# Router products by row tile inside the output projection, and earlier loads of the first four experts' weights, in a one-core streaming encoder layer

## The chip, the core and the metric

The kernel runs on one core of one Trainium2 chip. A core has a matrix engine (TensorE, PE in the profile), three elementwise engines (VectorE or DVE, ScalarE or ACT, GpSimd or POOL), and a sync engine (SyncE, SP) that here only issues transfers. Each has its own instruction queue and they meet at semaphores. The core has 16 DMA engines between HBM and the on-chip memory (SBUF); products land in PSUM, whose eight banks hold 512 fp32 columns each. The metric is the device time of one execution in microseconds, lower is better. All data is fp32.

## The reference

One encoder layer for 528 prompt rows (16 learned meta rows and 512 new ones) and 32 sample rows; two attention branches run ahead of what follows. The change is in the last part of it:

```python
def layer_tail(x, o_sb, o_dsa, g_sb, g_dsa, w_sb_branch, w_dsa_branch, w_out, norm2_g, ...):
    merged = (g_sb * (o_sb.reshape(B, L, SB_WIDTH) @ w_sb_branch)
              + g_dsa * (o_dsa.reshape(B, L, DSA_WIDTH) @ w_dsa_branch))
    h = x + merged @ w_out                       # w_out 1024 x 1024
    return h + hier_moe(rms_norm(h, norm2_g), ...)

def hier_moe(h, w_group, w_router, w_gate, w_up, w_down):
    group_probs = softmax(xt @ w_group)          # 4 groups, the best one is taken
    elog = xt @ w_router                         # 32 experts, the best 2 of 8 in that group
    ...                                          # weights of the two experts of each row
    a, b = xt @ w_gate[e], xt @ w_up[e]          # per expert 1024 x 256 each
    hh = silu(a) * b * comb
    y += hh @ w_down[e]                          # 256 x 1024
```

The meta rows are dropped from the result, so this part runs over 544 rows: 512 prompt rows in four tiles of 128, and one tile of 32 sample rows. The 32 experts' weights are 3 MiB each (gate 1 MiB, up 1 MiB, down two halves of 512 KiB), 96 MiB in all, and each is read once.

## The kernel before

The order of the work is written out by hand, engine by engine, with semaphores between.

**End of the attention.** TensorE fills the sparse attention's steps with 32 products of the gates and of one branch (`branch_products`, L1078, counted by `gd_ready`, 48 in all), then runs the sparse branch's projection (`by_width`, 16 jobs). DVE gates and adds them into `merged` (`merged_ready` counts 16). POOL then issues the loads of the residual rows X (`xres_in`) and of the norm gains `g2b` (`g2_in`).

**Output projection and second norm.** For each row tile t of 128 rows TensorE runs two jobs of 8 products, `merged` turned as the stationary operand and half of `w_out` (512 columns) as the moving one (`pj_job`, L747); the 32-row tile is packed four wide (L1218). Jobs go round four PSUM banks (`pj_wait_free`, the table `PJ` says which engine empties which job). DVE adds each job onto X (L2033, L2040, then `h_ready`), ACT squares and sums the row (L1547, `ss2_ready`), POOL takes the inverse root (L1620, L1621, `rstd2_ready`), and DVE writes the normed rows into `x2row` (L2020, `x2_ready`), a pair of buffers. DVE's program has the norm of tile t-1 behind the adds of tile t. TensorE turns the normed rows (`tr_job`, L737, two jobs of four transposes), with a lag of two tiles: tile u = t-2 behind the projection of tile t. ACT copies them into `xT`, which holds all 544 rows (L1355).

**Router.** When tile 3 is turned, one product runs over 512 rows at once: `wr` (36 columns: 4 groups, 32 experts) stationary, `xT` moving (L747). Another does the 32 sample rows. Their result has the experts on the partitions, so ACT copies it to `lgT` (L1557), TensorE turns it back (L1239), and ACT copies it to `rl` (L1560, `logits_ready`). DVE then picks groups and experts and builds lists of rows (L2070 to L2155), TensorE counts positions and makes the index lists (L1247 to L1256), and POOL gathers the first expert's rows (L1746).

**Experts.** Rows go through the experts in blocks of 64. For expert n, TensorE turns the gathered rows (L1266), multiplies with gate and up (L1273, `gu_ready`), turns the hidden rows (L1279) and multiplies with down (L1284, `y_done`). Weights sit in `MS` = 6 slots. SP loads expert n >= 6 into its slot when expert n-6 has left it: gate and up (L680) after `gu_ready` of n-6, the two down halves (L684) after `y_done` of n-6. The first six are loaded earlier: expert 0 behind `w_out` (L557) after the attention (`pvd_done`), expert 1 after `merged_ready`, experts 2 to 4 when the output projection is done, expert 5 after `logits_ready`, its last half after `slots_ready`.

Of the kernel before, what the change touches and what calls it, by code (L numbers as in the profile page):

```python
# [25 lines left out]
D = 1024  # L26
# [23 lines left out]
MS = 6  # L50
# [185 lines left out]
def build(nc, a, out):  # L236
    ctx = ExitStack()
    with ctx:
# [83 lines left out]
        moe_w = [arena[:, s * SLOT:(s + 1) * SLOT] for s in (2, 3, 0, 1)]  # L322

        Xg = ring_w[0:CAP, 0:2 * D].rearrange("p (i d) -> p i d", i=2)
        Yb = ring_w[:, 2 * D:3 * D].rearrange("p (i d) -> p i d", i=2)
        xgT = ring_w[:, 3 * D:4 * D].rearrange("p (i k s) -> p i k s", i=2, k=KT)

        moe_gu = [w[:, 0:4096] for w in moe_w] + [arena[:, 4 * SLOT:4 * SLOT + 4096], xnT[:, 0:4096]]
        moe_dn = [[w[:, 4096 + D * j:4096 + D * (j + 1)] for j in range(2)] for w in moe_w]
        moe_dn += [[ring_w[:, (6 + j) * D:(7 + j) * D] for j in range(2)], [ring_w[:, 5 * D:6 * D], tabs[:, 0:D]]]  # L330
        hid = ring_w[:, 4 * D:4 * D + 256].rearrange("p (i c) -> p i c", i=2)
        sil = ring_w[:, 4 * D + 256:4 * D + 512].rearrange("p (i c) -> p i c", i=2)
        hidT = ring_w[:, 4 * D + 512:4 * D + 768].rearrange("p (i c) -> p i c", i=2)
        lgT = tabs[:, 640:1200]

        x2row = ring_w[:, 0:2 * D].rearrange("p (i d) -> p i d", i=2)
        g2b = ring_w[:, 2 * D:3 * D]
        scrap = ring_w[:, 3 * D:4 * D]
# [28 lines left out]
        at_slot = ring_w[:, 0:2 * NT * CAP].rearrange("p (c s) -> p c s", s=CAP)  # L367
        at_block = ring_w[:, 640:640 + 2 * NT * NBLK].rearrange("p (c b) -> p c b", b=NBLK)
# [103 lines left out]
        logits_ready = sem("logits_ready")  # L472
# [41 lines left out]
        chunk_at = [wslot[s] for s in slots] + [arena[:, 0:4096], arena[:, 4096:8192]]  # L514


        pj_used = {0: 5, 1: 10, 2: 15, 3: 20, 4: 28, 5: 36, 9: 52, 12: 61, 13: 61}
# [5 lines left out]
        held_by = {2: 0, 3: 1, 4: 2, 5: 3, 6: 4, 7: 5, 8: 6, 10: 7, 11: 8, 9: 10}  # L523
# [40 lines left out]
        PJ = ["dve"] * 15 + ["act"] * (NT + 16) + ["dve"] * 16 + ["dve"] * 9 + ["act"] * 2  # L564
        J_IQ, J_SM, J_DQ, J_SV, J_SK, J_SQ = 0, 5, 10, 15, 20, 28
        J_B, J_WO, J_RT = 36, 52, 61

        TR = ["dve"] * 10 + ["act"] * 8 + ["act"] * 20 + ["act"] * 11
# [24 lines left out]
        RG = [(0, SEQ), (SEQ, NTOK)]  # L593
# [5 lines left out]
        def _(sp):  # L599
# [87 lines left out]
            for n in range(NE):  # L687
                s = n % MS
                if n == 1:
                    sp.wait_ge(merged_ready, 16)  # L690
                if n == 2:
                    sp.wait_ge(pj_ready, pj_used[13])
                if n == 5:
                    sp.wait_ge(logits_ready, 1)
                if n >= MS:
                    sp.wait_ge(gu_ready, n - MS + 1)
                load_gate_up(s, n, gu_in[s])
                if n >= MS:
                    sp.wait_ge(y_done, n - MS + 1)
                for j in range(2):  # L700
                    if n == 5 and j:
                        sp.wait_ge(slots_ready, 1)
                    load_down(s, n, j, dn_in[s])
# [23 lines left out]
        def _(pe):  # L727
# [477 lines left out]
            for t in range(NT + 2):  # L1205
# [17 lines left out]
                u = t - 2  # L1223
                if u >= 0:
# [4 lines left out]
                    if u >= NT - 2:  # L1229

# [560 lines left out]
        def _(dve):  # L1791
# [8 lines left out]
            for p in pairs:  # L1800
                link(nc.vector.memset(p[:, :], 0.0))
# [441 lines left out]
```

## Time and profile before

| | us |
|---|---|
| median of 3 runs | 937.8 |
| lowest, highest | 935.15, 939.65 |
| the profiled execution | 936.06 |
| its span | 934.3 |

| stretch, us from the span's start | what runs |
|---|---|
| up to 545.9 | projections, both attentions, branch projections |
| 545.9 to 606.5 | output projection |
| 606.5 to 625.6 | last turns, router |
| 625.6 to 656.9 | choice of experts, index lists, first gather, first gate and up product |
| 656.9 to 890.5 | experts, until the last weights have landed |
| 890.5 to the end | last two experts, scatter, sum, store |

The profiled execution took 936.06 us, of which the span from the first to the last instruction is 934.3 us. TensorE is busy for 827.5 us of it; the mean granted TensorE clock is 0.958 of full speed. The share of busy time is a mean over stages with different limits; which wait ends last has to be read stage by stage.

### The profile page before, as it was taken

To read this page: it belongs to the slowest core of one execution; us is meant where nothing else is said; L and a number is where in the kernel's file an instruction comes from. 1 tells how busy PE (TensorE), PEld (TensorE's weight loads), DVE (VectorE), ACT (ScalarE), POOL (GpSimd) and SP (SyncE) were. 2 spreads that over 40 slices of the span, in tenths; PEclk is the share of its full clock that TensorE was granted. 3 is DMA by queue.
4 is the path that set the end of the run, shared out by engine and by line. 5 is a ranking of instruction groups with operands and counts; after the bars stand their busy time and mean duration, and the time that the engine had idled before them with its cause. 6 is when DMAs were issued, how large, how long until landed. Compare 5 with 4: busy or idle time off the path is not lost.

```text
span 934.3 us, 11345 instructions
## 1 busy us (share of the span) xinstructions
PE 827.5 (89%) x4438; PEld 505.5 (54%) x4438; DVE 306.3 (33%) x788; ACT 224.0 (24%) x461; POOL 187.9 (20%) x257
## 2 busy tenths in 40 slices
PE   5999999999999998999999999953999988777870
PEld 3464344787666755766666854522555545444530
DVE  4213657996544421223222622235000000000005
ACT  3021331112333332343333500120122211111110
POOL 2223420000423212000000020101244332233230
PEclk9999999999999999999999999975999999999995
DMA  8424020422102001202040851195799999999927
GB/s 284 136 91 121 2 91 1 140 102 87 43 0 85 8 1 38 59 3 89 0 91 2 313 231 45 46 387 201 276 395 391 389 394 381 395 388 396 388 77 290
DMA packets 52422, 160.13 MB, mean 171 GB/s; under 512 B 14032, under 2 KB 16304, under 8 KB 43632
## 3 DMA queue, kind: packets, MB, share of 16 engines
q1 hardware_dynamic: 45184, 145.34, 42.0%
q0 software_dynamic: 7184, 14.06, 4.4%
q8 instruction: 35, 0.57, 0.3%
q14 instruction: 19, 0.16, 0.1%
HBM read 151.35 MB, written 15.86 MB: 179 GB/s over the span
## 4 chain that ended last, share of the span: by engine, by line
PE 70%; DMA 11%; SPq 6%; DVE 4%; POOL 3%; ACT 2%; issue 2%; POOLq 0%; DVEq 0%; ACTq 0%
PE quad L747 24%; PE pair L1078 9%; DMA arena<-in_w_up 6%; PE pair L941 5%; PE pair L1273 4%; PE quad L1273 3%; PE quad L815 3%; DMA xnT<-in_w_up 3%; SPq L680 3%; SPq L684 3%; PE quad L1284 2%; PE pair L737 2%; PE quad L1035 2%; POOL arena L1705 1%; PE pair L862 1%
## 5 line engine op out<-in xcount | busy, mean ns | idle before, releaser
L1273 PE MATMUL quad<-arena,ring_w 128*64 128x256 f32 x512 | 65.4, 413 | 16.5 <-DMA arena<-in_w_up 15.8
L747 PE MATMUL quad<-ring_w,xnT 128*128 128x512 f32 (+1 forms) x192 | 79.4, 554 | 0.0
L1750 POOL DMA_INDIRECT y_d<-ring_w,idx_y x64 | 57.7, 901 | 70.5 <-ACT ring_w L1584 58.4
L941 PE MATMUL pair<-xnT,ring_w 128*128 128x272 f32 x256 | 70.3, 410 | 0.9 <-POOLq L1711 0.9
L1078 PE MATMUL pair<-xnT,ring_w 128*128 128x272 f32 x256 | 65.8, 403 | 0.0
L1273 PEld LDWEIGHTS quad<-arena,ring_w 128*64 128x64 f32 x512 | 41.9, 149 | 35.3 <-issue 20.9
L747 PE MATMUL quad<-xnT,ring_w 128*128 128x280 f32 (+1 forms) x256 | 60.6, 396 | 0.0
L1746 POOL DMA_INDIRECT ring_w<-xn_d,idx_x x32 | 30.9, 966 | 137.4 <-PE pair L1266 53.7
L747 PE MATMUL quad<-arena 128*128 128x512 f32 x128 | 55.4, 593 | 1.2 <-DVEq L2012 1.2
L941 PEld LDWEIGHTS pair<-xnT,ring_w 128*128 128x128 f32 x256 | 46.4, 192 | 16.7 <-issue 7.9
L1078 PEld LDWEIGHTS pair<-xnT,ring_w 128*128 128x128 f32 x256 | 46.5, 189 | 15.3 <-issue 6.9
L747 PEld LDWEIGHTS quad<-xnT,ring_w 128*128 128x128 f32 x256 | 48.2, 190 | 11.3 <-issue 0.8
L1989 DVE CUSTOM_DVE_ANT_0 arena<-quad,arena 128x528 f32<-128x528 f32 (+4 forms) x34 | 17.7, 520 | 103.9 <-PE quad L1133 60.9
L747 PEld LDWEIGHTS quad<-ring_w,xnT 128*128 128x128 f32 x192 | 34.3, 189 | 31.7 <-issue 26.1
L1273 PE MATMUL pair<-arena,ring_w 128*64 128x256 f32 x352 | 42.1, 393 | 8.5 <-DMA arena<-in_w_up 8.1
L1921 DVE MAX8 small<-arena 128x8 f32<-128x544 f32 (+4 forms) x81 | 45.0, 555 | 2.2
L1923 DVE MATCH_REPLACE8 arena<-small,arena 128x544 f32<-128x544 f32 (+4 forms) x81 | 43.5, 537 | 0.0
L747 PEld LDWEIGHTS quad<-arena 128*128 128x128 f32 x128 | 24.2, 190 | 31.3 <-issue 29.7
L1273 PEld LDWEIGHTS pair<-arena,ring_w 128*64 128x64 f32 x352 | 27.1, 141 | 20.1 <-issue 8.7
L1730 POOL DMA_DIRECT2D hreg<-in_x_prompt x4 | 2.1, 536 | 173.6 <-DVEq L2012 173.6
L1078 PE MATMUL pair<-hreg,ring_w 128*128 128x272 f32 x128 | 33.0, 404 | 1.9 <-ACT arena L1498 1.8
L1948 DVE TENSOR_SCALAR arena<-quad 128x288 f32<-128x288 f32 (+6 forms) x22 | 16.0, 726 | 56.7 <-issue 37.9
(254 smaller groups left out, 1174.0 us busy)
## 6 DMA issues: line engine op xcount, KB each, us to landing
arena<-in_w_gate SPq DMA_DIRECT2D x27, 1024.0 KB, 16.9
arena<-in_w_up SPq DMA_DIRECT2D x27, 1024.0 KB, 25.4
arena<-in_w_down SPq DMA_DIRECT2D x44, 512.0 KB, 17.7
ring_w<-in_w_in SPq DMA_DIRECT2D x8, 2048.0 KB, 8.2
ring_w<-in_w_down SPq DMA_DIRECT2D x15, 512.0 KB, 17.9
xnT<-in_w_gate SPq DMA_DIRECT2D x5, 1024.0 KB, 17.7
xnT<-in_w_up SPq DMA_DIRECT2D x5, 1024.0 KB, 26.6
arena<-in_w_out SPq DMA_DIRECT2D x2, 2048.0 KB, 11.0
```

Source lines behind the costliest of these rows:

```text
L680: sp.dma_start(moe_gu[slot][:, n * 2048:(n + 1) * 2048], w[bass.ds(e * P, P), :])\
L684: sp.dma_start(moe_dn[slot][j], wd[:, bass.ds(e * 2 + j, 1), :].rearrange("p o c -> p (o c)"))\
L737: last = nc.tensor.transpose(b[0:cols, i * n:i * n + src.shape[0]], src, idn)
L747: last = nc.tensor.matmul(o, l, r, start=i == 0, stop=i == len(mms) - 1)
L815: last = nc.tensor.matmul(bank[t], xT[:, k, N_META + P * t:N_META + P * (t + 1)], chunk8(0)[:, k, :], start=k == 0, stop=k == KT - 1)
L941: last = nc.tensor.matmul(bank[6 + job % 2][:, 0:hi - lo], chunk8(6 + cb // 4)[:, k, c0:c0 + P], xT[:, k, lo:hi], start=k == 0, stop=k == ...
L1078: last = nc.tensor.matmul(bank[6 + job % 2][:, 0:hi - lo], w[:, k, c0:c0 + P], rhs[:, k, lo:hi], start=k == 0, stop=k == kt - 1)
L1273: last = nc.tensor.matmul(bank[4 * q + 1][64 * f:64 * f + 64, 0:256].rearrange("p (g c) -> p g c", g=2), xgT[:, q, k, :], wv[:, :, k, P * ...
L1746: pool.indirect_dma_start(Xg[:, q, :], None, xn2_d, bass.IndirectOffsetOnAxis(ap=rows, axis=0), bounds_check=NTOK - 1, oob_is_err=False).t ...
L1750: pool.indirect_dma_start(y_d, bass.IndirectOffsetOnAxis(ap=rows, axis=0), Yb[64 * c:64 * c + 64, q, :], None, bounds_check=4 * NTOK - 1, ...
L1921: link(nc.vector.max(top8, v))
L1923: link(nc.vector.match_replace(v, top8, v, TAKEN))
```

## The change

- TensorE's loop over the tiles is written anew. Behind the projection of tile t stands first the router product of tile t-2 (`routed`), then the turning of tile t-1: the turning lags one tile instead of two. The router product now has the turned rows stationary and `wr` (36 columns) moving, so that rows come out on the partitions; it is five jobs, one for each tile. The two wide products, the copies to `lgT` and the five transposes back are gone.
- The turned rows go into a pair of buffers `x2T` instead of `xT`. ACT copies each router result straight into `rl`.
- ACT's squares are written to a PSUM pair instead of SBUF. DVE sets the unused part of `rl` to zero at the start of the program.
- `w_out` is loaded into `xnT` and the first half of `ring_w`, when the gate products are done with them (`held_by`), instead of into the arena. Gate and up of experts 0 to 3 follow after `pvd_done`; their down halves when the branch projection is done, five of the eight after `merged_ready`; experts 4 and 5 when the output projection is done. From expert 6 on the waits are as before.
- `x2row`, `g2b` and small buffers of the expert loop move within `ring_w` and `tabs`.

The core of the diff:

```diff
-        chunk_at = [wslot[s] for s in slots] + [arena[:, 0:4096], arena[:, 4096:8192]]
+        chunk_at = [wslot[s] for s in slots] + [xnT[:, 0:4096], wslot[0]]
...
-        held_by = {2: 0, 3: 1, 4: 2, 5: 3, 6: 4, 7: 5, 8: 6, 10: 7, 11: 8, 9: 10}
+        held_by = {2: 0, 3: 1, 4: 2, 5: 3, 6: 4, 7: 5, 8: 6, 10: 7, 11: 8, 9: 10, 12: 11, 13: 11}
...
-            for n in (7, 8, 10, 11, 9):
+            for n in (7, 8, 10, 11, 9, 12, 13):
                 load_chunk(sp, n)
-            sp.wait_ge(pvd_done, NT)
-            load_chunk(sp, 12)
-            load_chunk(sp, 13)
...
+            sp.wait_ge(pvd_done, NT)
+            for n in range(4):
+                load_gate_up(n, n, gu_in[n])
+            sp.wait_ge(pj_ready, pj_used[9])
+            for n in range(4):
+                for j in range(2):
+                    if (n, j) == (1, 1):
+                        sp.wait_ge(merged_ready, 16)
+                    load_down(n, n, j, dn_in[n])
+            sp.wait_ge(pj_ready, pj_used[13])
+            for n in range(4, MS):
+                load_gate_up(n, n, gu_in[n])
+                for j in range(2):
+                    load_down(n, n, j, dn_in[n])
...
-            for t in range(NT + 2):
+            def routed(t):
+
+                pe.wait_ge(tr_free_act, emptied(TR, "act", T_X2 + 2 * t + 1))
+                pj_job([(x2T[:, t % 2, k, 0:TOK[t]], wr[:, k, :]) for k in range(KT)], lambda b: b[0:TOK[t], 0:36])
+
+            for t in range(NT + 1):
...
-                u = t - 2
-                if u >= 0:
+                if t == 2:
+                    pe.wait_ge(wr_in, 32)
+                if t >= 2:
+                    routed(t - 2)
+                if t >= 1:
+                    u = t - 1
                     pe.wait_ge(x2_ready, u + 1)
...
+            routed(NT - 1)
...
-                    link(nc.scalar.activation(scrap[0:r, :], X[0:r, t, :], ACT.Square, scale=1.0 / 32.0,
+
+                    link(nc.scalar.activation(pair67[0:r, :], X[0:r, t, :], ACT.Square, scale=1.0 / 32.0,
...
-            dve.wait_ge(logits_ready, 1)
+            dve.wait_ge(pj_free_act, emptied(PJ, "act", J_RT[NT - 1]))
```

TensorE's queue from the output projection to the router, before. `quad<-arena 128x512` is the projection (48 are the six jobs of tiles 0 to 2), `pair<-cst,ring_w` the turning of normed rows, `quad<-xnT,small` the router:

```order
L747 MATMUL quad<-arena,ring_w 128x272 x64
L747 MATMUL quad<-arena 128x512 x48
L737 MATMUL pair<-cst,ring_w 128x128 x8
L747 MATMUL quad<-arena 128x512 x16
L737 MATMUL pair<-cst,ring_w 128x128 x8
L1218 MATMUL quad<-arena 32x256 x32
L737 MATMUL pair<-cst,ring_w 128x128 x16
L747 MATMUL quad<-xnT,small 36x512 x8
L737 MATMUL pair<-cst,ring_w 128x32 x8
L747 MATMUL quad<-xnT,small 36x32 x8
L1239 MATMUL pair<-cst,tabs 128x36 x4
L1239 MATMUL pair<-cst,tabs 32x36
```

The same place in the changed program, from the second half of tile 1's projection to the turning of tile 2. The projection of a tile is now a row of 8 that reads `xnT` and one that reads `ring_w`; `quad<-small,ring_w` is a router product:

```order
L745 MATMUL quad<-ring_w,arena 128x512 x8
L735 MATMUL pair<-cst,ring_w 128x128 x8
L745 MATMUL quad<-xnT,arena 128x512 x8
L745 MATMUL quad<-ring_w,arena 128x512 x8
L745 MATMUL quad<-small,ring_w 128x36 x8
L735 MATMUL pair<-cst,ring_w 128x128 x8
L745 MATMUL quad<-xnT,arena 128x512 x8
L745 MATMUL quad<-ring_w,arena 128x512 x8
L745 MATMUL quad<-small,ring_w 128x36 x8
L735 MATMUL pair<-cst,ring_w 128x128 x8
```

The turning of tile 0 stands between the projections of tiles 1 and 2, where there was nothing, and two router products stand ahead of the last projection. The end of the same stretch, changed program, from the last products of the 32-row tile on:

```order
L1221 MATMUL quad<-ring_w,arena 32x256 x2
L745 MATMUL quad<-small,ring_w 128x36 x8
L735 MATMUL pair<-cst,ring_w 128x128 x8
L745 MATMUL quad<-small,ring_w 128x36 x8
L735 MATMUL pair<-cst,ring_w 128x32 x8
L745 MATMUL quad<-small,ring_w 32x36 x8
L1242 MATMUL quad<-rt,cst 128x192
```

Behind the last projection there are now three router products and the turning of two tiles, before three tiles were turned there and the wide router products followed. SP's queue from `w_out` to the last load that is not yet under the loop's waits, before:

```order
L557 DMA arena<-in_w_out 128x8x512 [waits pvd_done]
L557 DMA arena<-in_w_out 128x8x512
L680 DMA arena<-in_w_gate 128x2048
L680 DMA arena<-in_w_up 128x2048
L684 DMA arena<-in_w_down 128x1024 x2
L680 DMA arena<-in_w_gate 128x2048 [waits merged_ready]
L680 DMA arena<-in_w_up 128x2048
L684 DMA arena<-in_w_down 128x1024 x2
L680 DMA arena<-in_w_gate 128x2048 [waits pj_ready]
```

and in the changed program, from the fourth expert's gate on:

```order
L672 DMA arena<-in_w_gate 128x2048
L672 DMA arena<-in_w_up 128x2048
L676 DMA arena<-in_w_down 128x1024 [waits pj_ready]
L676 DMA arena<-in_w_down 128x1024 x2
L676 DMA arena<-in_w_down 128x1024 [waits merged_ready]
L676 DMA arena<-in_w_down 128x1024 x4
L672 DMA arena<-in_w_gate 128x2048 [waits pj_ready]
L672 DMA arena<-in_w_up 128x2048
L676 DMA ring_w<-in_w_down 128x1024 x2
L672 DMA xnT<-in_w_gate 128x2048
```

Two experts' weights are now left for the time after the output projection, where there were four.

## Rows read from the trace of the kernel before

**Rows 1.** Windows: us, busy (x) of PE, PEld, DVE, ACT, POOL, PEclk, DMA share, GB/s.
```profile
650.00:656.00 6.00, 5.31 (x33) 3.28 (x34) 0.00 (x0) 0.60 (x1) 0.94 (x1) 0.58 0.13 38
656.00:662.00 6.00, 5.57 (x49) 3.58 (x45) 0.58 (x2) 0.87 (x2) 0.93 (x1) 1.00 0.71 246
662.00:668.00 6.00, 6.00 (x47) 3.39 (x45) 0.58 (x2) 1.47 (x3) 2.03 (x3) 1.00 0.73 233
656.90:890.50 233.60, 204.77 (x1430) 120.32 (x1430) 17.36 (x60) 43.54 (x89) 79.28 (x86) 0.97 1.00 383
```
**Rows 2.** SP's timeline: start us, us, what it issues.
```profile
656.91 0.33 SPq L680 DMA_DIRECT2D arena<-in_w_gate  x1
...
665.18 0.80 SPq L684 DMA_DIRECT2D arena<-in_w_down  x2
```
**Rows 3.** TensorE's timeline, branch projection to router; in brackets idle before and releaser.
```profile
515.25 29.50 PE L747 MATMUL quad<-arena,ring_w 128*128 128x272 f32 x128
545.93 41.47 PE L747 MATMUL quad<-arena 128*128 128x512 f32 x96 [1.18 <-DVEq L2012]
587.23 1.04 PE L737 MATMUL pair<-cst,ring_w 128*128 128x128 f32 x8
588.11 13.90 PE L747 MATMUL quad<-arena 128*128 128x512 f32 x32
...
602.82 3.66 PE L1218 MATMUL quad<-arena 128*32 128x256 f32 x64
606.41 1.16 PE L737 MATMUL pair<-cst,ring_w 128*128 128x128 f32 x8
610.47 1.88 PE L737 MATMUL pair<-cst,ring_w 128*128 128x128 f32 x8 [2.89 <-ACT xnT L1355]
613.08 9.21 PE L747 MATMUL quad<-xnT,small 128*36 128x512 f32 x16 [0.73 <-issue]
622.22 1.06 PE L737 MATMUL pair<-cst,ring_w 32*128 32x32 f32 x8
623.69 0.72 PE L747 MATMUL quad<-xnT,small 128*36 128x32 f32 x16 [0.41 <-issue]
```
**Rows 4.** DVE's timeline: adds (L2033) and norms (L2020), then the choice (L2070).
```profile
564.12 1.53 DVE L2033 TENSOR_TENSOR hreg<-quad,hreg 128x512 f32<-128x512 f32 x2 [18.31 <-DMA ring_w<-in_norm_g]
587.43 0.69 DVE L2033 TENSOR_TENSOR hreg<-quad,hreg 128x512 f32<-128x512 f32 x1 [6.18 <-PE quad L747]
588.37 1.28 DVE L2020 SCALAR_TENSOR_TENSOR ring_w<-hreg,small,ring_w 128x1024 f32<-128x1024 f32 x1 [0.25 <-DVE hreg L2033]
608.61 1.28 DVE L2020 SCALAR_TENSOR_TENSOR ring_w<-hreg,small,ring_w 128x1024 f32<-128x1024 f32 x1 [0.35 <-DVE hreg L2040]
611.89 1.27 DVE L2020 SCALAR_TENSOR_TENSOR ring_w<-hreg,small,ring_w 32x1024 f32<-32x1024 f32 x1 [1.99 <-POOL small L1621]
625.61 0.18 DVE L2070 TENSOR_REDUCE small<-small 128x5 f32<-128x20 f32 x1 [11.51 <-ACT small L1560]
```
**Rows 5.** Timeline of TensorE's weight loads, at the turn of tile 3.
```profile
610.43 1.51 PEld L737 LDWEIGHTS pair<-cst,ring_w 128*128 128x128 f32 x8 [3.05 <-DVE ring_w L2020]
```
**Rows 6.** TensorE's timeline in the first attention: short products, and a wait.
```profile
332.86 0.51 PE L1043 MATMUL quad<-arena,cst 128*128 128x16 f32 x4
333.22 0.70 PE L941 MATMUL pair<-xnT,ring_w 128*128 128x272 f32 x2
336.39 0.47 PE L998 MATMUL pair<-arena 128*64 128x144 f32 x4 [1.79 <-POOLq L1711]
```
**Rows 7.** Windows, columns as in the first group: clock behind two waits, and elsewhere.
```profile
337.00:341.00 4.00, 4.00 (x13) 2.83 (x10) 0.58 (x1) 0.00 (x0) 0.41 (x1) 0.57 0.02 4
545.90:606.50 60.60, 60.57 (x209) 28.22 (x209) 9.38 (x11) 6.77 (x12) 9.72 (x20) 1.00 0.31 119
610.00:618.00 8.00, 6.80 (x15) 2.74 (x16) 1.91 (x6) 2.00 (x4) 1.97 (x4) 0.57 0.99 367
49.00:56.00 7.00, 5.10 (x38) 3.73 (x35) 0.55 (x3) 4.55 (x9) 1.09 (x2) 1.00 0.80 286
```

More of the change, by code:

```diff
@@ L321, in build @@
         wslot = [ring_w[:, s * 4096:(s + 1) * 4096] for s in range(2)]
[L322 to L338, printed above, removed]
+        Xg = ring_w[0:CAP, 4 * D:6 * D].rearrange("p (i d) -> p i d", i=2)
+        Yb = ring_w[:, 6 * D:7 * D].rearrange("p (i d) -> p i d", i=2)
+        xgT = ring_w[:, 7 * D:8 * D].rearrange("p (i k s) -> p i k s", i=2, k=KT)
+        hid, sil, hidT = (tabs[:, 512 + 256 * i:768 + 256 * i].rearrange("p (i c) -> p i c", i=2) for i in range(3))
+        moe_gu = [arena[:, D * u:D * (u + 4)] for u in (0, 4, 11, 15, 24)] + [xnT[:, 0:4 * D]]
+        moe_dn = [[arena[:, D * u:D * (u + 1)] for u in units] for units in ((8, 9), (10, 19), (20, 21), (22, 23))]
+        moe_dn += [[ring_w[:, D * u:D * (u + 1)] for u in units] for units in ((0, 1), (2, 3))]
+        x2row = ring_w[:, 4 * D:6 * D].rearrange("p (i d) -> p i d", i=2)
+        x2T = ring_w[:, 6 * D:8 * D].rearrange("p (i k r) -> p i k r", i=2, k=KT)
+        g2b = tabs[:, 0:D]
         so = [0]
@@ L685, in load_down @@
                     .then_inc(arrived, 16)
-            for n in range(NE):
-                s = n % MS
[L689 to L696, printed above, removed]
+            sp.wait_ge(pvd_done, NT)
[12 more added lines that the diff above has]
+                    load_down(n, n, j, dn_in[n])
+            for n in range(MS, NE):
+                s = n % MS
+                sp.wait_ge(gu_ready, n - MS + 1)
                 load_gate_up(s, n, gu_in[s])
-                if n >= MS:
-                    sp.wait_ge(y_done, n - MS + 1)
+                sp.wait_ge(y_done, n - MS + 1)
                 for j in range(2):
-                    if n == 5 and j:
-                        sp.wait_ge(slots_ready, 1)
                     load_down(s, n, j, dn_in[s])
@@ L1228, in _ @@
                         tr_job([(xk[:, 4 * q + i, :], ident[0:TOK[u], 0:TOK[u]]) for i in range(4)], TOK[u])
-                    if u >= NT - 2:
-                        pe.wait_ge(wr_in, 32)
-                        pe.wait_ge(tr_free_act, emptied(TR, "act", T_X2 + 2 * u + 1))
-                        lo, hi = RG[u - (NT - 2)]
-                        pj_job([(wr[:, k, :], xT[:, k, lo:hi]) for k in range(KT)], lambda b: b[0:36, 0:hi - lo])
-            pe.wait_ge(pj_free_act, emptied(PJ, "act", len(PJ) - 1))
-            tr_wait_free(pe, tr[0])
-            for t in range(NT):
-                last = nc.tensor.transpose(bank[4 + tr[0] % 2][0:TOK[t], 36 * t:36 * (t + 1)],
-                                           lgT[0:36, TOFF[t]:TOFF[t] + TOK[t]], ident[0:36, 0:36])
-            last.then_inc(tr_ready, 1)
+            routed(NT - 1)
             pe.wait_ge(onehot_ready, 1)
```

33 lines of the change are left out of this document (15 added, 18 removed).

## The prediction

> **What bounds the kernel now.** I read the page first: TensorE is busy for most of the span, but an average says nothing of a stage, so windows come next. From 656.9 to 890.5 us the DMA engines are busy all the time at 383 GB/s [rows 1]: this stretch is as long as its bytes. 26 experts of 3.15 MB are 81.8 MB; 383 GB/s over 233.6 us are 89.5 MB, the rest being gathers and scatters. It begins when the first gate and up product releases a slot (656.91), and its first down load waits until 665.18 [rows 2]. Just before it the DMA engines idle: 38 GB/s in the six us from 650 [rows 1], since all six slots are full. So the end of the program is the start of the first gate and up product plus a constant, and loads that come earlier than now land in slots that are full in time anyway. What can move the end is the chain from the end of the branch projection (545.9) to 656.9. Its first part is TensorE without a gap up to the end of the output projection [rows 3], its second the turns and the router, where TensorE, DVE and ACT wait for each other, its third the choice of experts on DVE from 625.61 [rows 4]. The third is untouched, so I ask only how far DVE's start at 625.61 moves.
>
> **The loads.** Both programs hold six experts and start the seventh by the same wait. In the changed one the 12.6 MB of `w_out` and four gates and ups start near 516 us (the gate products' end, 515.25 [rows 3]) and take 33 us at 383 GB/s, to about 549; 4.2 MB of down halves and 2.75 MB of residual and gains follow (18 us, to 567). Experts 4 and 5, 6.3 MB, need 16 us from the projection's end and are there before 650. Gain of the loads: nothing. Their possible price: DVE's first add waits for residual and gains until 564.12 [rows 4]; that is 2.5 us behind the bytes then due (5.9 MB from 546.2, 561.6), so I expect 568, and 569.6 if theirs come last. The norm of tile 0 is wanted at 574.6 and follows DVE's start by some 4 us (two adds, square, root), so this costs nothing up to about 570.7, and one for one beyond.
>
> **The turns inside the projection.** Now take the new place of a turn. A projection job's last product is behind when TensorE could issue at 587.23 [rows 3]; DVE's add starts at 587.43, its norm of the tile before ends at 588.37 + 1.28 = 589.65 [rows 4]; from such a norm's end (608.61 + 1.28 = 609.89) to the weight load that it releases, 0.54 us go by (610.43) [rows 4, 5]. So a turn that stands right behind a projection can start 589.65 + 0.54 - 587.23 = 2.96 us after it; with a lag of two tiles it waited for nothing. The norm doesn't need the new adds, but DVE's program has them ahead of it. The turn itself takes 588.11 - 587.23 = 0.88 us. Each gap is 3.84 us, and there are three: behind tiles 1, 2 and 3. In the second and third a router product stands first. Its 8 products are 16 records, as every fp32 product here; the nearest row with a 128-column stationary operand and few columns is 4 records in 333.22 - 332.86 = 0.36 us, 90 ns each [rows 6], so 1.44 us. Were it 190 ns, as in 1.51/8 of a weight load at half clock [rows 5], it would be 3.0 us: both fit in the 2.96 us wait, so inside the gaps it is free. Three gaps, 11.5 us, less the two turns that stood in the projection already (0.88 each), are **+9.8 us** until the last projection's end, which was at 606.41, when the next turn could be issued [rows 3].
>
> **The clock in the gaps.** The first gap has TensorE idle for 2.8 us. Before, an idle of 2.89 us [rows 3] was followed by a granted clock of 0.57 over 8 us [rows 7], that is 6.9 us at 1.2 GHz (2 x 0.43 x 8); an idle of 1.79 us [rows 6] by 0.57 over 4 us, 3.4 us [rows 7]; one of 1.18 us, at 545.93 [rows 3], by none (1.00 up to 606.5 [rows 7]). Half of such a time is lost: 1.7 or 3.4 us. I take the middle, **+2.6 us**. The second and third gaps idle for 1.5 us, between the row with a fall and the one without; I take no fall, and price it below.
>
> **Behind the last projection.** Before, from its end to DVE's start: 625.61 - 606.41 = 19.2 us. Changed: the turn of tile 3 can't start before 4.0 us (610.43 again [rows 5]: its norm waits for the packed adds). At 2.4 GHz it ends at 5.0, the second copy needs 0.7 (the turn of 610.47 ended at 612.35, the next product came at 613.08), the router product 1.4: 7.2. The last norm ends at 611.89 + 1.27 [rows 4], 6.75 after the projection, and 0.54 on the small turn starts, at 7.3; it takes 1.06, then 0.4 for its copy (622.22 + 1.06 to 623.69), 0.7 for the last product (0.72 for 16 records), 0.4 for copy and DVE: 9.8 us, 9.4 less than before. But the wait for the norm leaves 2.5 us of idle, as before, and the clock fell there. With 3.4 us at 1.2 GHz the chain is 11.1, with 6.9 us 12.6: gains of 8.1 and 6.6. I take **-7.3 us**. What goes is mostly the 9.21 us product [rows 3], which ran partly at 1.2 GHz, and the way back through `lgT`.
>
> **Sum.** 9.8 + 2.6 - 7.3 = +5.1 us, on the profiled execution 936.1 + 5.1 = 941.2. That execution lies 1.7 below the median of 937.8; on the median it is 942.9, which I predict. Zeroing `rl` costs 0.1 us at the start at most, squares into PSUM cost as before: DVE and ACT have time there.
>
> **A rule against the row.** In the stretch from 49 to 56 us nearly all that TensorE does is transposes with short waits, and the granted clock is 1.00 [rows 7]. The Trainium skill, "TensorE: Matmul & The Clock Gate", section "Part 4: PE-mode transpose", says that transposes don't count as TensorE being busy for the clock gate. By that rule each of the three gaps is nearly 3.8 us of nothing and the clock falls in each, which is rival 1; by the row it need not.
>
> **Rivals.** (1) The clock falls in all three gaps. For it: the gaps are 3.84 us with only 1.4 us of very short products and a turn. Against it: the clock of 1.00 in the stretch above. Price over the forecast: 3.4 for tile 3's projection by the larger row, 3.6 for the packed one (3.66 us of work, all at half speed), 0.8 and 0.7 for the upper values of the terms above: +13.6, 951.4; with the smaller falls about +9.6, 947.4. (2) The clock stays at 2.4 GHz in every gap and behind the projection. For it: 1.18 us of idle didn't lower it. Against it: 1.79 and 2.89 us did, and the first gap is 2.8. Sum 9.8 - 9.4 = +0.4, 938.2: no difference. This is the case that ends as not slower; it decides from the point where what the clock costs, in the gaps and at the end together, is under 4.3 us (4.7 less 0.4). (3) Faster: the early loads matter after all. For it: SP waited, and from 662 to 668 there were only 233 GB/s [rows 1], so the stream starts lame; if the queue were fed there, the 1.7 MB that are missing in the twelve us from 656 (137 and 150 GB/s for six us each) are 4.5 us. With rival 2 that gives 933.7, the edge of faster. Against it: this hole is the wait for `y_done` of expert 0 (665.18), which the change keeps. (4) The residual lands late: 19.5 MB from 516 on are 51 us at 383 GB/s; were the rate 6% lower, 569.6 becomes 572.7, 2 us beyond the limit of 570.7, and the sum +7.1, 944.9. For it: two queues share the engines. Against it: 3.1 us must be lost.
>
> **How the numbers follow.** A measurement can tell about 0.5%, 4.7 us, from no change. Forecast 0.45, a little over half of it above 942.5; rival 1 0.25; rival 2 0.19; rival 3 0.07; rival 4 0.04. Slower: 0.24 + 0.25 + 0.03 = 0.52; faster 0.07; same the rest, 0.41. The forecast's own range is 939.5 (9.8 + 1.7 - 8.1 = +3.4, less the 1.7 of the base) to 944.4 (9.8 + 3.4 - 6.6 = +6.6). The range goes from 937.0, rival 2 with part of the base's 1.7, to 950.0, most of rival 1.
>
> **What would show it.** The trace of after should show, behind the projections of tiles 1, 2 and 3, turns that wait for DVE's norm, with 2.8 us of idle at the first; a clock of 1.2 GHz in the first microseconds of tile 2's projection; router products of 1.4 us (3.0 would add 1.5 at the end); the last projection's end at 617 to 620 instead of 606.41; DVE's choice 11 to 12.6 us behind that; first gate and up product ended at about 662; then 233 us of full DMA. Wrong it would be if the turns don't wait, if the choice starts before 625, or if the stretch of full DMA is shorter than 230 us.

## The result

| | before | after |
|---|---|---|
| median of 12 runs, us | 937.68 | 942.69 |
| lowest, highest | 935.15, 939.65 | 939.06, 946.84 |
| ratio of the times, 95% interval | | 1.0053 (1.0033 to 1.0074) |
| profiled execution, its span | 936.06, 934.3 | 945.74, 943.9 |

The changed kernel is 0.5% slower, 5.0 us by the medians. The forecast was 942.9. The two profiled executions differ by more, 9.7 us; 4.1 of that lies ahead of the output projection, as will be seen.

### The profile after

TensorE's timeline of the changed kernel (start us, us, engine and line, operation, operands, count; in brackets idle before it and what ended it), from the start of the output projection to the first gate and up product, answers to [rows 3]:

```profile
550.07 7.13 PE L745 MATMUL quad<-xnT,arena 128*128 128x512 f32 x16 [1.18 <-DVEq L2006]
...
570.78 7.03 PE L745 MATMUL quad<-ring_w,arena 128*128 128x512 f32 x16
580.12 1.93 PE L735 MATMUL pair<-cst,ring_w 128*128 128x128 f32 x8 [2.31 <-DVE ring_w L2014]
581.85 7.96 PE L745 MATMUL quad<-xnT,arena 128*128 128x512 f32 x16
589.64 7.03 PE L745 MATMUL quad<-ring_w,arena 128*128 128x512 f32 x16
596.51 1.87 PE L745 MATMUL quad<-small,ring_w 128*128 128x36 f32 x16
598.99 1.16 PE L735 MATMUL pair<-cst,ring_w 128*128 128x128 f32 x8 [0.61 <-DVE ring_w L2014]
599.99 7.03 PE L745 MATMUL quad<-xnT,arena 128*128 128x512 f32 x16
...
613.73 1.87 PE L745 MATMUL quad<-small,ring_w 128*128 128x36 f32 x16
616.31 1.16 PE L735 MATMUL pair<-cst,ring_w 128*128 128x128 f32 x8 [0.71 <-DVE ring_w L2014]
...
620.99 1.98 PE L745 MATMUL quad<-small,ring_w 128*128 128x36 f32 x16
624.53 1.96 PE L735 MATMUL pair<-cst,ring_w 128*128 128x128 f32 x8 [1.57 <-DVE ring_w L2014]
627.18 3.62 PE L745 MATMUL quad<-small,ring_w 128*128 128x36 f32 x16 [0.69 <-ACT ring_w L1350]
...
659.67 6.60 PE L1268 MATMUL quad<-arena,ring_w 128*64 128x256 f32 x32 [0.69 <-ACT ring_w L1566]
```

All three turns inside the projection wait for DVE's norm, 2.31 us where nothing else stands in the gap and 0.61 and 0.71 us where a router product of 1.7 us is ahead. The next two rows of DVE show why, beside [rows 4]: an add of tile 2 (L2027) stands ahead of the norm of tile 1 (L2014), although the norm does not read it.

```profile
596.71 0.69 DVE L2027 TENSOR_TENSOR hreg<-quad,hreg 128x512 f32<-128x512 f32 x1 [6.17 <-PE quad L745]
597.65 1.28 DVE L2014 SCALAR_TENSOR_TENSOR ring_w<-hreg,small,tabs 128x1024 f32<-128x1024 f32 x1 [0.25 <-DVE hreg L2027]
...
633.68 0.17 DVE L2064 TENSOR_REDUCE small<-small 128x5 f32<-128x20 f32 x1 [5.00 <-ACT small L1550]
```

Windows of the same trace (us, busy (x) of PE, PEld, DVE, ACT, POOL, granted clock, DMA share, GB/s), which answer to [rows 7] and [rows 1]:

```profile
580.00:584.00 4.00, 3.88 (x11) 2.67 (x12) 0.06 (x1) 1.20 (x2) 1.43 (x3) 0.57 0.32 131
596.00:600.00 4.00, 3.39 (x27) 2.96 (x26) 1.98 (x2) 1.61 (x4) 0.69 (x2) 1.00 0.00 0
613.00:618.00 5.00, 4.29 (x39) 3.39 (x41) 1.98 (x2) 2.29 (x5) 1.29 (x3) 1.00 0.06 25
626.00:632.00 6.00, 5.13 (x27) 4.52 (x25) 1.91 (x6) 1.49 (x5) 0.90 (x2) 0.50 1.01 360
650.00:656.00 6.00, 2.37 (x20) 2.21 (x20) 3.04 (x9) 0.00 (x0) 1.12 (x2) 0.50 0.00 1
666.30:899.90 233.60, 206.06 (x1430) 120.70 (x1430) 17.39 (x60) 43.52 (x89) 78.45 (x85) 0.96 1.00 382
```

The clock fell to 1.2 GHz behind the first gap (3.4 us at 1.2 GHz: 2 x 0.43 x 4), not in the second or third, and again behind the last projection. The DMA engines stood still from 650 to 656 and then moved 382 GB/s over 233.6 us, where before they moved 383 [rows 1]: the stretch of weights is the same, it only begins later.

### Where the time went

Four points cut the program the same way in every trace of this study: the first product of the output projection, the first instruction behind the last one, DVE's choice of experts, and SP's issue of expert 6 when the first gate and up product ends. Lengths in us, from the profiled executions:

| kernel | projection starts | projection | to DVE's choice | to expert 6's load | to the span's end | median of runs |
|---|---|---|---|---|---|---|
| before | 545.93 | 60.5 | 19.2 | 31.3 | 277.4 | 937.7 |
| after | 550.07 | 70.9 | 12.7 | 32.6 | 277.6 | 942.7 |
| after_again | 546.20 | 70.9 | 12.3 | 31.3 | 277.5 | 940.0 (one run) |

The change lost 10.4 us in the projection and won 6.5 behind it, +3.9 (in the second trace +3.5). The 4.1 us at the start are chance. The second trace of the same kernel has them not, and over all thirteen traces of this study the projection starts between 545.93 and 550.07: 545.9 to 549.7 in the four that have the old order of TensorE's work, 546.2 to 550.1 in the nine that have a new one. The difference is there already when the branch projection starts (515.25 before, 519.40 after). The 1.3 us of the fourth part are chance too: the first gate and up product takes 5.42 us before, 6.60 after and 5.39 in after_again by the clock that it finds, and 6.59 in `before_copy_first` below, which has the router of before. The last part is a constant.

### The profile page after: what moved, and what is told of

It reads as the page before. It is cut to its first block, busy times and chain, and to the rows that moved or that the text cites. A ratio compares the mean times of both kernels' runs of the same rounds, so it can differ in the third digit from the quotient of the medians.

```text
span 943.9 us, 11436 instructions
## 1 busy us (share of the span) xinstructions
PE 833.5 (88%) x4481; PEld 516.2 (55%) x4481; DVE 306.7 (32%) x789; ACT 224.2 (24%) x463; POOL 188.3 (20%) x257
## 4 chain that ended last, share of the span: by engine, by line
PE 68%; SPq 10%; DMA 9%; DVE 5%; POOL 3%; issue 2%; ACT 2%; POOLq 0%; DVEq 0%
PE quad L745 24%; PE pair L1076 9%; DMA arena<-in_w_up 6%; SPq L672 5%; PE pair L939 5%; SPq L676 4%; PE pair L1268 3%; PE quad L813 3%; PE quad L1268 3%; PE pair L735 2%; PE quad L1033 2%; POOL arena L1698 2%; PE quad L1279 2%; PE pair L860 1%; DMA arena<-y_d 1%
## 5 line engine op out<-in xcount | busy, mean ns | idle before, releaser
L1268 PE MATMUL quad<-arena,ring_w 128*64 128x256 f32 x512 | 63.2, 403 | 13.4 <-DMA arena<-in_w_up 12.7
L1076 PEld LDWEIGHTS pair<-xnT,ring_w 128*128 128x128 f32 x256 | 46.5, 189 | 15.3 <-issue 6.9
L813 PE MATMUL quad<-ring_w,xnT 128*128 128x512 f32 x64 | 31.5, 644 | 2.9 <-DMA ring_w<-in_w_in 2.9
L1505 ACT ACTIVATE arena<-arena,small 128x528 f32<-128x528 f32 (+4 forms) x34 | 19.6, 577 | 51.1 <-DVEq L1987 51.1
```

The source lines that it names most:

```text
L813: last = nc.tensor.matmul(bank[t], xT[:, k, N_META + P * t:N_META + P * (t + 1)], chunk8(0)[:, k, :], start=k == 0, stop=k == KT - 1)
L1076: last = nc.tensor.matmul(bank[6 + job % 2][:, 0:hi - lo], w[:, k, c0:c0 + P], rhs[:, k, lo:hi], start=k == 0, stop=k == kt - 1)
L1268: last = nc.tensor.matmul(bank[4 * q + 1][64 * f:64 * f + 64, 0:256].rearrange("p (g c) -> p g c", g=2), xgT[:, q, k, :], wv[:, :, k, P * ...
L1505: ins = nc.scalar.activation(v, v, ACT.Exp, scale=HD ** -0.5, bias=nbias[:, i % DR, u:u + 1], accum_out=rsum[:, i % DR, u:u + 1])
```

## Experiments

Each kernel's edit is given against the one it is named after; all but `before_norm_first`, `before_both_first` and `before_copy_first` are edits of the changed kernel. There are eleven runs beside the two, one of them the changed kernel unaltered. A median is set against that of the kernel before from the same session, which is why the second number varies from 936.9 to 938.3.

### Is it DVE's queue order that makes the gaps?

`norm_first`, the changed kernel with the norm ahead of the adds (DVE's loop):

```diff
             for t in range(NT + 1):
+                if t:
+                    second_norm(t - 1)
                 if t < NT:
...
                     nc.vector.sem_inc(h_ready, 1)
-                if t:
-                    second_norm(t - 1)
```

> The changed kernel with one edit: in DVE's program the norm of tile t-1 stands ahead of the adds of tile t, not behind them. Theory A (the gaps in TensorE come from DVE's queue order: the norm waits behind adds that it does not need): the waits of 2.3, 2.5 and 2.6 us behind the projections of tiles 1, 2 and 3 go, the output projection takes about 65 us instead of 70.9, the clock stays at 2.4 GHz in it, and from the last projection's end to DVE's choice there are 8 to 9.5 us instead of 12.7; median about 932, 11 below the changed kernel. Rival B (the gaps are the length of the chain add, square, root, norm itself): the turns still wait about as long, median 942 +-2.

Measured: 933.7 us against 936.9, ratio 0.9971 (0.9957 to 0.9986), 9.0 us under the changed kernel by the medians, 7.7 by the two ratios, 9.1 by the traces (74.5 us from the projection's start to the choice instead of 83.6). Projection 64.9, then 9.6 us to the choice. The turn that waited 2.31 us now follows the projection at once:

```profile
571.80 3.60 PE L745 MATMUL quad<-ring_w,arena 128*128 128x512 f32 x8
575.23 1.05 PE L735 MATMUL pair<-cst,ring_w 128*128 128x128 f32 x8
576.12 4.46 PE L745 MATMUL quad<-xnT,arena 128*128 128x512 f32 x10
```

Theory A holds for the gaps: the chain from add to norm fits beside a tile's projection, it was only queued behind the wrong instructions. What is left at the end is a wait for ACT, whose copies (L1350) stand behind the square of the last tile (L1543):

```profile
614.64 1.02 ACT L1543 ACTIVATE pair<-hreg 32x1024 f32<-32x1024 f32 x1 [4.63 <-DVEq L2040]
...
616.01 1.08 ACT L1350 ACTIVATE ring_w<-pair 128x512 f32<-128x512 f32 x2
...
617.15 2.17 PE L745 MATMUL quad<-small,ring_w 128*128 128x36 f32 x16 [1.61 <-ACT ring_w L1350]
```

`norm_first` with ACT's order mended too was not run.

`lag_two` goes the other way and takes the need for an early norm away. TensorE's and ACT's programs have the turns two tiles behind the projection and the router products three; DVE's is untouched. TensorE's part of the edit:

```diff
-            for t in range(NT + 1):
+            for t in range(NT + 2):
...
-                if t >= 2:
-                    routed(t - 2)
-                if t >= 1:
-                    u = t - 1
+                if t >= 3:
+                    routed(t - 3)
+                if t >= 2:
+                    u = t - 2
```

> The changed kernel with its turns and router products one tile later in TensorE's and ACT's programs: turns lag two tiles as before the change, router products three. DVE's program as in the changed kernel. Theory A (the lag of one tile makes the gaps): no wait in the projection, which takes 60.5 + 1.7 us (one router product stands in it), clock 1.00; behind it four router products and three turns, with ACT's copies held by the square as before, 14 to 16 us instead of 12.7; sum about 5 to 7 us under the changed kernel, median about 936. Rival (the short products themselves are what costs): as the changed kernel, 942.

Measured: 937.7 against 937.8, ratio 0.9997 (0.9987 to 1.0008): 5.0 us under the changed kernel, 937.7 where 936 was expected. Projection 62.3, as expected, then 16.5 to the choice, where 14 to 16 were. So the gaps need both the lag of one tile and the norm's place behind the adds: taking either away removes them. The short product that still stands in the projection costs what its duration says, 62.3 against 60.5 + 1.7. Behind it the clock fell again, after a wait of 1.61 us for ACT's copies; the turn then took 1.95 us, where 1.13 us is its time at 2.4 GHz (613.80 in the same trace):

```profile
616.53 3.03 PE L745 MATMUL quad<-small,ring_w 128*128 128x36 f32 x16 [1.61 <-ACT ring_w L1350]
619.37 1.95 PE L735 MATMUL pair<-cst,ring_w 128*128 128x128 f32 x8
```

### What does the clock cost?

`filled`, the changed kernel with unused products in two of the waits (three behind tile 1, two behind the first router product at the end):

```diff
+                if t in (1, NT - 1):
+                    pj_wait_free(pe, pj[0])
+                    for i in range(3 if t == 1 else 2):
+                        nc.tensor.matmul(bank[pj[0] % 4][:, :], ident, cst[:, 0:512],
+                                         start=True, stop=True)
                 if t >= 1:
                     u = t - 1
```

> The changed kernel with products whose result is not used where TensorE waits for a norm: three of 512 columns behind tile 1's projection, two behind the first router product after the last projection. Nothing else is moved. Theory A (1.2 GHz is granted because of these waits, and costs about 1.7 us in the projection and 2.8 at the end): the granted clock stays 1.00 from tile 1 to the last router product, output projection 69.2 us instead of 70.9, end part about 10 instead of 12.7, median about 938.2. Rival D (the clock falls anyway, by the short turns and router products): no change, 942.7, clock as in the changed kernel.

Measured: 940.2 against 936.9, ratio 1.0029 (1.0012 to 1.0046), some 2.5 us under the changed kernel, less than the 4.5 expected. The parts came as Theory A said: projection 69.3, then 10.3 to the choice. TensorE's timeline at the end, where the turn took 1.96 us and the router product 3.62 in the changed kernel:

```profile
620.80 1.96 PE L1233 MATMUL quad<-cst 128*128 128x512 f32 x4
622.60 1.09 PE L735 MATMUL pair<-cst,ring_w 128*128 128x128 f32 x8
624.42 1.98 PE L745 MATMUL quad<-small,ring_w 128*128 128x36 f32 x16 [0.73 <-ACT ring_w L1355]
```

The granted clock was 1.00 from 549 to 627 us. So it fell because of the waits, and the falls cost 1.7 us in the projection and 2.4 at the end, 4.1 us in these traces. The medians show 2.5 and the two ratios 2.3; with intervals of about 0.2% on either side of each ratio, the 4.1 is neither confirmed nor excluded.

### Do the early loads do anything?

`loads_old`, the changed kernel with nearly the loads of before. `w_out` stays where the change put it, and expert 5 is loaded with experts 2 to 4 instead of after the router:

```diff
             sp.wait_ge(pvd_done, NT)
-            for n in range(4):
-                load_gate_up(n, n, gu_in[n])
-            sp.wait_ge(pj_ready, pj_used[9])
-            for n in range(4):
-                for j in range(2):
-                    if (n, j) == (1, 1):
-                        sp.wait_ge(merged_ready, 16)
-                    load_down(n, n, j, dn_in[n])
-            sp.wait_ge(pj_ready, pj_used[13])
-            for n in range(4, MS):
+            load_gate_up(0, 0, gu_in[0])
+            sp.wait_ge(pj_ready, pj_used[9])
+            for j in range(2):
+                load_down(0, 0, j, dn_in[0])
+            sp.wait_ge(merged_ready, 16)
+            load_gate_up(1, 1, gu_in[1])
+            for j in range(2):
+                load_down(1, 1, j, dn_in[1])
+            sp.wait_ge(pj_ready, pj_used[13])
+            for n in range(2, MS):
```

> The changed kernel with the experts' weights loaded as in the kernel before: expert 0 ahead, expert 1 after the merge, experts 2 to 5 when the output projection is done. Theory A (all six slots are full before the first gate and up product in either case, so the early loads gain nothing): median 942.7 +-1.5, the stretch of full DMA begins at the first gate and up product's end as before. Rival E (the early loads pay, and without them the change would lose more): 4 us or more slower, 947.

Measured: 941.6 against 936.9, ratio 1.0043 (1.0030 to 1.0056), beside 1.0053 for the changed kernel. The early loads of the experts gain nothing that can be measured; what the earlier place of `w_out` does was not tried alone. `loads_late` asks for the other side:

```diff
             sp.wait_ge(pj_ready, pj_used[13])
+            sp.wait_ge(slots_ready, 1)
             for n in range(4, MS):
```

> The changed kernel with experts 4 and 5 loaded only when the slots of the rows are known (slots_ready), about 29 us later: 6.3 MB then run from about 650 to 667, where the DMA engines idled. Theory A (what counts is only that slots are full when their turn comes, and the DMA engines idle before the first gate and up product anyway): within 2 us of the changed kernel. Rival E (each us of earlier loading counts): 16 us slower.

Measured in one run: 948.5, and a span of 946.7. Both theories miss: 5.8 us over the changed kernel, not within 2 and not 16. TensorE never waited for these loads (no such wait from 640 to 760 us), but the first gather did; TensorE's wait for its rows:

```profile
661.74 1.14 PE L1262 MATMUL quad<-cst,ring_w 64*128 64x64 f32 x8 [8.80 <-DMA ring_w<-xn_d,idx_x]
```

The window of the same trace in which the gather is on its way, with the DMA engines' share and GB/s last:

```profile
656.00:662.00 6.00, 0.26 (x2) 0.26 (x3) 0.00 (x0) 0.00 (x0) 0.69 (x1) 0.50 1.03 348
```

The changed kernel has a wait of 4.69 us there, though POOL issued its gather no earlier (654.57 us; 654.36 here, where the loads went out from 650.61 on). So 4.1 us were lost to 6.3 MB that ran through the same DMA engines as a gather of 64 rows, and from the issue of expert 6 at 669.85 to the end there are 276.9 us, as everywhere. Loads need not be early for the slots, but they must be out of the way of the small transfer on the chain.

### What held the turn at the end, before the change?

`before_norm_first` is the kernel before with the same edit of DVE's loop as `norm_first`.

> The kernel before with the same one edit in DVE's program. Theory A: the projection is as long as before (60.5 us), the turn of tile 3 no longer waits behind the packed adds, the wide router product runs at 2.4 GHz (6.9 us instead of 9.2), from the last projection's end to DVE's choice about 13.5 us instead of 19.2; median about 932, the same as norm_first within 2 us: then the router by tiles is worth nothing in itself. Rival C (taking the wide product and the way back off the end is what pays, once the waits are gone): norm_first is 4 us or more faster than this one.

Measured: 937.3 against 936.9, ratio 0.9995 (0.9980 to 1.0009). No gain at all, a clear miss, and the trace names what I had read wrongly. DVE's norm is done at 609.27, 4 us before the turn it releases; what comes last is ACT. ACT's, DVE's and TensorE's rows:

```profile
607.98 1.29 DVE L2020 SCALAR_TENSOR_TENSOR ring_w<-hreg,small,ring_w 128x1024 f32<-128x1024 f32 x1 [2.48 <-POOL small L1621]
...
611.20 1.05 ACT L1547 ACTIVATE ring_w<-hreg 32x1024 f32<-32x1024 f32 x1 [3.17 <-DVEq L2046]
...
612.48 1.08 ACT L1355 ACTIVATE xnT<-pair 128x512 f32<-128x512 f32 x2
...
613.22 1.94 PE L737 MATMUL pair<-cst,ring_w 128*128 128x128 f32 x8 [2.89 <-ACT xnT L1355]
```

The turn of tile 3 needs the banks of tile 2's turn. ACT's copies out of them (L1355) stand behind the square of the last tile (L1547), which waits for DVE's packed adds. Two kernels test this. `before_both_first` adds to the edit above the same in ACT's loop, `before_copy_first` has the ACT edit alone:

```diff
+                u = t - 2
+                if u >= 0:
+                    for q in range(2):
+                        tr_copy(xT[:, 4 * q:4 * q + 4, TOFF[u]:TOFF[u] + TOK[u]], 4, TOK[u])
                 if t < NT:
                     r = TOK[t]
                     act.wait_ge(h_ready, t + 1)
...
                     nc.scalar.sem_inc(ss2_ready, 1)
-                u = t - 2
-                if u >= 0:
-                    for q in range(2):
-                        tr_copy(xT[:, 4 * q:4 * q + 4, TOFF[u]:TOFF[u] + TOK[u]], 4, TOK[u])
```

> The kernel before with two edits: DVE's norm of tile t-1 ahead of the adds of tile t, and in ACT's program the copies of the turned tile t-2 ahead of the square of tile t. before_norm_first left TensorE's wait of 2.89 us behind the last projection as it was, so Theory F now: that wait was ACT's queue order (the copies that free the turns' banks stand behind a square that waits for the packed adds), not DVE's norm. Then here both are gone: the turn of tile 3 starts within 1 us of tile 2's, the clock stays at 2.4 GHz, the wide router product takes 6.9 us instead of 8.9, from the last projection's end to DVE's choice 13 to 14 us instead of 19.2; median about 932. Rival: something else holds the turn, 937 as before.

> The kernel before with ACT's edit alone. Theory F says that either order alone holds the turn of tile 3: with ACT's mended, it starts at the end of DVE's norm, 3.4 us behind the last projection instead of 4.0; the wait is 2.3 instead of 2.9 us, the rest as before, 936.5. Rival (ACT's order alone was the cause): the turn starts about 1 us behind the last projection's end, 932.

Measured: `before_both_first` 935.0 against 937.8, ratio 0.9965 (0.9953 to 0.9978); `before_copy_first` 937.3 in one run. TensorE in the first, then in the second:

```profile
610.17 1.16 PE L737 MATMUL pair<-cst,ring_w 128*128 128x128 f32 x8
611.66 1.14 PE L737 MATMUL pair<-cst,ring_w 128*128 128x128 f32 x8 [0.33 <-ACT xnT L1355]
615.06 7.03 PE L747 MATMUL quad<-xnT,small 128*36 128x512 f32 x16 [2.26 <-issue]
```

```profile
611.79 1.16 PE L737 MATMUL pair<-cst,ring_w 128*128 128x128 f32 x8 [2.38 <-DVE ring_w L2020]
613.72 8.38 PE L747 MATMUL quad<-xnT,small 128*36 128x512 f32 x16 [0.78 <-issue]
```

With both orders mended the wait is 0.33 us and the wide product runs at 2.4 GHz in 7.03 us; with one of them the turn waits for the other engine, 2.38 us, as Theory F said. From the last projection's end to the choice are 15.3 us in the first (13 to 14 expected) and 17.2 in the second, instead of 19.2. The miss of 1.3 us in the first is the 2.26 us ahead of the wide product: the edit puts the square between two pairs of copies, and now the second pair stands behind it.

### What is the router by tiles worth, and what is left?

`lag_two_both_first` is `lag_two` with both orders mended.

> lag_two with DVE's norm ahead of the adds and ACT's copies ahead of the square. Nothing should wait behind the last projection for longer than a copy: projection 62.2 us, then 10.5 to 12 us to DVE's choice, clock 1.00 until then; 6 to 8 us under the kernel before, median about 930. If work on TensorE and not its waits is what is left, it equals norm_first (933.7) within 2 us.

Measured: 934.0 against 937.8, ratio 0.9969 (0.9953 to 0.9984), the same as `norm_first` at 0.9971 and `before_both_first` at 0.9965. Three programs with the router in three places come out alike once their waits are short; by their traces, from the projection's start to the span's end, they take 384.7 us (`norm_first`), 383.6 (`before_both_first`) and 385.2 (this one). So the router by tiles is worth nothing here that can be measured. Two limits go with that: each interval is some 1.4 us wide to either side, so a difference under 2 us would not be seen, and each of the three still has something left that could be mended (1.61 us, 2.26 us, a fall of the clock). The likely reason, argued from the order of the work, is that the change moves TensorE's work from the end into the projection, where TensorE is just as much on the chain. The end part took 14.6 us, not the 10.5 to 12 expected, and the windows show a clock that falls without a long wait:

```profile
608.00:610.00 2.00, 2.00 (x28) 1.50 (x20) 1.91 (x3) 0.00 (x0) 0.34 (x1) 1.00 0.37 57
610.00:612.00 2.00, 1.57 (x14) 1.38 (x13) 0.95 (x3) 0.84 (x2) 0.26 (x1) 1.00 0.75 279
612.00:614.00 2.00, 1.70 (x16) 1.70 (x17) 0.00 (x0) 1.35 (x4) 0.43 (x2) 1.00 1.04 336
614.00:616.00 2.00, 2.00 (x11) 1.64 (x10) 1.39 (x3) 0.60 (x1) 0.36 (x1) 0.55 0.94 358
```

`norm_first_warm` is `norm_first` with unused products in the idle stretches between the last router product and the first gathered rows:

```diff
+            def warm(count):
+                for _ in range(count):
+                    nc.tensor.matmul(bank[2], ident, cst[:, 0:512], start=True, stop=True)
+
+            pe.wait_ge(pj_free_act, emptied(PJ, "act", len(PJ) - 1))
+            warm(8)
             pe.wait_ge(onehot_ready, 1)
             b = bank[0]
-            pe.wait_ge(pj_free_act, emptied(PJ, "act", len(PJ) - 1))
...
+            warm(7)
             pe.wait_ge(slots_ready, 1)
...
+            warm(4)
             pe.wait_ge(gath[0], 16)
```

> norm_first with products of 512 columns whose result is not used, behind the last router product (8), ahead of the index product (7) and ahead of the first gather's rows (4): TensorE has 8.4, 7.4 and 4.6 us of idle there, the products take 0.87 us each at 2.4 GHz. Theory G (the end is the first gate and up product's end plus a constant, and 1.2 GHz in that product, 6.0 us instead of 3.6, and in the index products, costs one for one): clock 1.00 from there on, gate and up 3.7 us, index products 1.2 instead of 2.4, together about 4.2 us less, median 929.5, and as long a stretch of full DMA behind it. Rival (the time there hangs on the gather and on DVE, or the stream of weights swallows the gain): 933.7.

Measured: 930.8 against 938.3, ratio 0.9921 (0.9906 to 0.9936), the fastest kernel of the study and faster than both. TensorE's rows:

```profile
620.70 9.09 PE L1240 MATMUL quad<-cst 128*128 128x512 f32 x16 [0.28 <-ACT small L1557]
629.63 0.84 PE L1247 MATMUL quad<-rt,cst 128*128 128x192 f32 x2
...
638.47 1.37 PE L1257 MATMUL quad<-ring_w 128*64 128x49 f32 x20 [1.42 <-DVEq L2156]
...
646.77 3.67 PE L1274 MATMUL quad<-arena,ring_w 128*64 128x256 f32 x32 [0.69 <-ACT ring_w L1573]
```

Gate and up took 3.67 us instead of 6.03. Against `norm_first` the gain is 2.9 us by the medians and by the traces from the projection's start to the span's end (381.9 against 384.7), 4.7 by the two ratios, which come from different sessions; 4.2 were expected. Part of what is missing in the trace is seen: the first eight products took 9.09 us, not 7, since the clock had fallen among the short turns and router products ahead of them (0.71 from 617 to 619 us) and was still 0.58 from 623 to 625, and so held up the counting product. It starts 8.9 us behind DVE's choice instead of 8.1, with no idle ahead of it.

`after_again` is the changed kernel unaltered.

> The changed kernel once more, for a second trace: where the output projection starts (550.07 in the first, 545.93 in the kernel before) and whether the clock falls behind tile 1 alone. Theory: the start is chance (waits and the clock in the attention), anywhere from 546 to 550; from there to DVE's choice 83.6 us +-1.5 as in the first trace, and 1.2 GHz in the first gap only. Rival: the change itself delays the start by 4 us.

Its row stands in the table above: start at 546.20, 83.2 us from there to the choice. In its first gap the fall was again there; the turn took 1.50 us and the next eight products 8.41.

The constant, last: from the issue of expert 6 to the span's end, 277.4 us before, 277.6 and 277.5 after, 278.2 in `norm_first` (654.18 to 932.4), 277.8 in `norm_first_warm` (650.49 to 928.3), 276.9 in `loads_late`. The start of that part moved by 19 us between these kernels, and its length by 1.3.

## Why the prediction was right, point by point

**The bound and the constant** were right, and `norm_first_warm` and `loads_late` show it from both sides. **The loads** gained nothing, as `loads_old` shows. Their possible price did not come due: DVE's first add came 21.0 us after the projection's start (571.08), where 22 were forecast and 24.8 was the limit.

**The gaps** were named rightly, with their cause, and sized a little too large: 3.84 us forecast for each; without the clock's part they took 3.35 (577.65 to 581.85, less 0.85), 3.48 (596.51 to 599.99) and 3.67. The term that failed is the 0.54 us from DVE's norm to the turn. In the row I took it from, the turn was released by ACT's copy, as its own bracket says [rows 3]; DVE's norm had only ended shortly before. Measured, the turn starts 0.06 us behind the norm (597.65 + 1.28 to 598.99). A router product takes 1.7 us (589.86 to 591.56 in `norm_first`, where no wait follows it), not 1.44, which the gaps hid as forecast. The projection became 10.4 us longer; the sum had 9.8 + 2.6.

**The clock.** It fell where forecast, in the first gap and at the end, and not in the other two. The first fall cost 1.8 us (0.85 in the turn, 0.9 in the projection), the lower of the two values between which I had taken the middle. In the second and third gap, about 3.5 us with a turn in each, it stayed at 1.00. By the rule of the Trainium skill that transposes do not count as busy in the same way ("TensorE: Matmul & The Clock Gate", "Part 4: PE-mode transpose") the prediction had it fall in all three, but that reading passed over the router product in the second and third: 1.7 us that are no transpose, with 0.6 to 0.7 us of idle. So these gaps do not test the rule; the row that speaks against it is the stretch of transposes from 49 to 56 us, at 1.00 [rows 7]. At the end of `lag_two_both_first` it fell behind waits of at most 0.73 us, among turns and thin products. The runs don't tell which of the two kinds weighs how much.

**The end** gained 6.5 us against the 7.3 taken, close to the 6.6 that went with the longer time at 1.2 GHz (how the chains of 11.1 and 12.6 us follow from the 9.8 the prediction does not work out), and that is what the trace shows: from the turn of tile 3 on the clock stays at 0.50. The reading behind it, that the turn of tile 3 waits for its norm, was right for the changed kernel (1.57 us, on DVE's L2014) and half right for the kernel before: there ACT's copy came last (it ends at 610.33, the norm at 609.89), and mending either order alone left the turn held by the other.

**The sum.** +3.9 and +3.5 us by the two traces up to the choice, +5.1 forecast, +5.0 by the medians (3.1 to 6.9 by the interval). That 942.9 meets 942.7 is in part luck: the projection's term was 2 us too high, the end's 0.8 too favourable, and the traces stay 1.2 to 1.6 us under the forecast sum. The rest between traces and medians is within what single executions scatter in the start of the projection and in the first gate and up product (5.4 to 6.6 us), and is not settled further. Of the signs named, the choice came 12.7 and 12.3 us behind the last projection (11 to 12.6 forecast) and 233.6 us of full DMA followed. The last projection's end at 620.99 lies outside 617 to 620 by the late start; it is 617.13 in `after_again`. Rivals 1, 2 and 4 are out by the traces (no fall in the later gaps, a fall in the first, no late residual), rival 3 by `loads_old`.

## What to carry to other kernels

It is not enough that an operation's inputs are ready in time; in its engine's program it must also stand ahead of whatever waits longer. A step that is moved closer to its producer should be followed through every engine that feeds it or frees its buffer: here one `if` of DVE's program cost 8 to 9 us, and in the kernel before DVE's and ACT's order each held the same turn, so that mending one alone gave nothing or little. And work moved from one part of a chain to another part of the same chain, on the engine that both parts wait for, gains only the waits that it removes, as far as the three kernels above can tell.

## What the runs showed of the hardware

- The granted clock can fall with TensorE busy nearly all the time: busy 5.27 of the 6.00 us from 608 to 614, ahead of the fall in `lag_two_both_first`, in a row of turns and products of 36 columns with no wait over 0.73 us.
- A product of 36 columns on a stationary operand of 128 takes 107 ns for each of its two records at 2.4 GHz (1.70 us for 16, 589.86 to 591.56 in `norm_first`) and 222 ns at 1.2 GHz (3.56 us for 16, 627.18 to 630.74 in the changed kernel).
- Unused products of 512 columns in idle stretches brought back 2.9 us of 934 by the medians (4.7 by the ratios), by keeping 2.4 GHz for the work behind them; started at 1.2 GHz they were late themselves and gave a part of it back.
- A gather of 64 rows whose rows TensorE waited 4.7 us for made it wait 8.8 us when the first of 6.3 MB of weights was issued 3.8 us before it (654.36 against 650.61), in one trace of each.
